# Recurrence mixer of a fused two-model block: gates and q/k square sums as rounded one-pass products, three convolution taps moved into the softmax

## What is computed

```python
h = _rmsnorm(x, norm_mix[l])
xr, gr, q, k, v, ga, gb = jnp.split(h @ w_in[l], splits, axis=-1)
xc = _centred_dwconv(xr, conv_w[l], conv_b[l])          # 4 taps along the sequence
h_fwd = _rglru_scan(xc, gates 0); h_bwd = flip(_rglru_scan(flip(xc), gates 1))
# in _rglru_scan: two block-diagonal products of xc (64x64 blocks) are the gates r and i,
#   a = exp(c*r*log_sigmoid), h[t] = a*h[t-1] + sqrt(1-a*a)*(i*xc)
y_lru = (h_fwd + h_bwd) * gelu(gr)
q = _rmsnorm(q per head) * q_norm * HEAD_DIM ** -0.5; k = _rmsnorm(k per head) * k_norm
y_att = _neighbourhood_attention(q, k, v, rel_pos_bias)  # softmax over 8 rows x 16 columns
y = sigmoid(ga) * y_lru + sigmoid(gb) * y_att
x = x + y @ w_out
```

## Time and profile before

| what | value |
|---|---|
| median of 3 runs | 2387.43 us (2387.39 to 2388.82) |
| span of the profiled execution | 2385.7 us, its first to its last instruction |
| PE, DVE, ACT, POOL busy | 99%, 54%, 42%, 7% of the span |
| one body of the loop | 51.2 us (the square sums of body 2 start at 511.07, of body 3 at 562.29) |

### The profile page before, as it was taken

How to read it: one execution, slowest core, us unless ns; L and a number is a source line. 1 busy time by engine, 2 the same in 40 slices (tenths; PEclk the granted TensorE clock), 3 DMA queues, 4 the chain that set the end, 5 groups by cost and what they waited for, 6 DMA issues and landing times.

```text
span 2385.7 us, 31197 instructions
## 1 busy us (share of the span) xinstructions
PE 2359.3 (99%) x11062; PEld 1904.2 (80%) x11062; DVE 1296.1 (54%) x1838; ACT 996.1 (42%) x1481; POOL 155.6 (7%) x137
## 2 busy tenths in 40 slices
PE   9999999999999999999999999999999999999998
PEld 8888887777777788888877778888877768888887
DVE  5444346566666734443364575555248996655424
ACT  4222224766666632232243444333234455433322
POOL 0000002434433000000000000000000000000000
PEclk9999999999999999999999999999999999999999
DMA  4333322223232232232232223333213222323321
GB/s 167 96 96 94 121 93 89 81 84 101 74 100 76 81 97 97 97 116 97 68 100 88 89 71 97 97 96 121 95 40 102 77 71 71 97 91 102 111 97 48
DMA packets 62185, 219.94 MB, mean 92 GB/s; under 512 B 7664, under 2 KB 12272, under 8 KB 62112
## 3 DMA queue, kind: packets, MB, share of 16 engines
q1 hardware_dynamic: 60944, 216.86, 28.1%
q10 hardware_dynamic: 1168, 2.12, 0.3%
HBM read 216.83 MB, written 2.12 MB: 92 GB/s over the span
## 4 chain that ended last, share of the span: by engine, by line
PE 84%; DVE 7%; ACT 5%; issue 3%; DMA 0%; ACTq 0%; DVEq 0%; SPq 0%
PE bank L1948 26%; PE bank L1950 26%; PE bank L1949 26%; DVE wL L1941 1%; ACT m_prob L242 1%; PE bank L598 1%; ACT wH L1936 1%; DVE m_prob L369 1%; PE bank L641 1%; PE bank L1042 0%; PE bank L1070 0%; PE bank L2344 0%; PE bank L2343 0%; PE bank L2342 0%; PE bank L1052 0%
## 5 line engine op out<-in xcount | busy, mean ns | idle before, releaser
L1948 PE MATMUL bank<-H,wH 128*128 128x512 f32 x2996 | 1183.4, 395 | 8.2 <-DVE L L2040 3.6
L1950 PE MATMUL bank<-H,wL 128*128 128x512 f32 x2996 | 1166.8, 389 | 0.0
L1949 PE MATMUL bank<-L,wH 128*128 128x512 f32 x2996 | 1166.5, 389 | 0.0
L1941 DVE TENSOR_TENSOR wL<-raw,wH 128x1024 fp32r<-128x1024 f32 (+1 forms) x359 | 468.5, 1312 | 610.6 <-ACT wH L1936 610.4
L1948 PEld LDWEIGHTS bank<-H,wH 128*128 128x128 f32 x2996 | 562.8, 188 | 137.5 <-issue 13.3
L1950 PEld LDWEIGHTS bank<-H,wL 128*128 128x128 f32 x2996 | 562.5, 188 | 118.7
L1949 PEld LDWEIGHTS bank<-L,wH 128*128 128x128 f32 x2996 | 562.8, 188 | 117.5 <-issue 4.1
L1936 ACT ACTIVATE wH<-raw 128x1024 fp32r<-128x1024 f32 (+1 forms) x359 | 394.9, 1108 | 215.2 <-PE bank L1950 206.0
L2158 ACT ACTIVATE H<-prod 128x512 f32 (+1 forms) x88 | 55.8, 634 | 243.8 <-DVE prod L2223 243.8
L2203 DVE TENSOR_TENSOR gate_s<-bank,rstd 128x512 f32<-128x512 f32 x88 | 60.8, 691 | 107.1 <-PE bank L1950 106.9
L2223 DVE TENSOR_TENSOR prod<-silu_g,bank 128x512 f32<-128x512 f32 x88 | 60.3, 685 | 80.1 <-PE bank L1950 74.0
(11 more groups left out here) (279 smaller groups left out, 1726.2 us busy)
## 6 DMA issues: line engine op xcount, KB each, us to landing
raw<-in_w_ffn_gu SPq DMA_DIRECT2D x88, 512.0 KB, 3.4
raw<-in_w_in SPq DMA_DIRECT2D x56, 512.0 KB, 3.6
raw<-in_w_ffn_down SPq DMA_DIRECT2D x32, 704.0 KB, 4.2
raw<-in_w_up_2a SPq DMA_DIRECT2D x44, 512.0 KB, 3.4
raw<-in_w_up_2b SPq DMA_DIRECT2D x44, 512.0 KB, 3.4
raw<-in_w_in_even SPq DMA_DIRECT2D x24, 512.0 KB, 4.4
raw<-in_w_in_odd SPq DMA_DIRECT2D x24, 512.0 KB, 3.5
raw<-in_w_down_2a SPq DMA_DIRECT2D x16, 704.0 KB, 4.2
```

The costliest lines, as they stand in the source:

```text
L1941: dve.tensor_tensor(w_l, raw_at(st, j), w_h.bitcast(F32), ALU.subtract).then_inc(S.lo_done, 1)
L1948: pe.matmul(out, w_h, xh[:, k0 + k], start=start and k == ks[0], stop=False)
L1949: pe.matmul(out, w_h, xl[:, k0 + k], start=False, stop=False)
L1950: last = pe.matmul(out, w_l, xh[:, k0 + k], start=False, stop=stop and k == ks[-1])
```

## The change

Three things. The gate products take rounded operands: ACT rounds the convolution result to `xcH` and the gate weights to `gwH`, DVE makes the remainders `xcL` and `gwL`, and each gate product becomes three one-pass products, as in `products`. The square sums become two one-pass products: ACT writes the square twice, once in float32 and once rounded (`sqH`), DVE subtracts (`sqL`), and the head matrix, which rounds exactly, is used rounded. And of the next body's convolution taps 0 and 1 now stand between `dve_scores(p, 2)` and `dve_scale(p, 2)`, tap 2 between `dve_scores(p, 3)` and `dve_scale(p, 3)`, and only tap 3 at the body's head. The new tiles lie over old ones (`over`), so DVE waits in body 0 for the gates before it writes `thb`.

```diff
+    def act_xc_high(act, p):
+        act.wait_ge(M.conv, 4 * p + 4)
+        wait(act, M.lru, 6 * p)
+        act.activation(xcH[:], xc[:], ACT.Copy).then_inc(M.gate_hi, 1)
+    def act_gw_high(act, p):
+        act.wait_ge(M.gw_loaded, 16 * p + 16)
+        wait(act, M.gab, 2 * p)
+        act.activation(gwH[:], gate_w[:], ACT.Copy).then_inc(M.gate_hi, 1)
...
                 act.activation(sqk[:, n], qk[:, n], ACT.Square).then_inc(M.sqk, 1)
+            if not first:
+                act_xc_high(act, p)
+            for n in range(2):
+                wait(act, M.qkn, 2 * p)
+                act.activation(sqH[:, n], qk[:, n], ACT.Square).then_inc(M.sqk, 1)
             slot(1)
...
             act_probT(act, p, 0)
+            act_gw_high(act, u)
             act_probs(act, p, 2)
...
         k.split_hi(act, st, 0, 4)
+        act.activation(heads1R[:], k.heads1[:], ACT.Copy).then_inc(M.gate_hi, 1)
+        act_gw_high(act, 0)
+        act_xc_high(act, 0)
...
+    def dve_xc_low(dve, p):
+        dve.wait_ge(M.gate_hi, 2 * p + 3)
+        dve.tensor_tensor(xcL[:], xc[:], xcH[:].bitcast(F32), ALU.subtract).then_inc(M.split_lo, 1)
+    def dve_gw_low(dve, p):
+        dve.wait_ge(M.gate_hi, 2 * p + 2)
+        dve.tensor_tensor(gwL[:], gate_w[:], gwH[:].bitcast(F32), ALU.subtract).then_inc(M.split_lo, 1)
+    def dve_sq_low(dve, p):
+        for n in range(2):
+            dve.wait_ge(M.sqk, 4 * p + n + 3)
+            dve.tensor_tensor(sqL[:, n], sqk[:, n], sqH[:, n].bitcast(F32), ALU.subtract).then_inc(M.split_lo, 1)
...
             if not first:
-                dve_conv(dve, p)
+                dve_conv(dve, p, (3,))
+                dve_xc_low(dve, p)
             slot(1)
...
                 dve_tail(dve, p - 1)
+            dve_sq_low(dve, p)
             if first:
                 dve_scaled(dve, 5)
...
             slot(6)
+            dve_gw_low(dve, p + 1)
             dve_lru(dve, p, 1)
             dve_scores(dve, p, 2)
+            dve_conv(dve, p + 1, (0, 1))
             dve_scale(dve, p, 2)
             dve_scores(dve, p, 3)
+            dve_conv(dve, p + 1, (2,))
             dve_scale(dve, p, 3)
...
         k.normal_dve(dve, site, 0, 3)
+        dve_gw_low(dve, 0)
+        dve_xc_low(dve, 0)
         dve_scaled(dve, 2)
...
-            pe.matmul(bank[4 + g][:], gate_w[:, 2 * d + g], xc[:], start=True, stop=True).then_inc(M.gates, 1)
+            pe.matmul(bank[4 + g][:], gwH[:, 2 * d + g], xcH[:], start=True, stop=False)
+            pe.matmul(bank[4 + g][:], gwH[:, 2 * d + g], xcL[:], start=False, stop=False)
+            pe.matmul(bank[4 + g][:], gwL[:, 2 * d + g], xcH[:], start=False, stop=True).then_inc(M.gates, 1)
...
-                pe.matmul(bank[6 + n][:], k.heads1[:], sqk[:, n], start=True, stop=True).then_inc(M.qk_stat, 1)
+                pe.matmul(bank[6 + n][:], heads1R[:], sqH[:, n], start=True, stop=False)
+                pe.matmul(bank[6 + n][:], heads1R[:], sqL[:, n], start=False, stop=True).then_inc(M.qk_stat, 1)
```

More of the change, by code:

```diff
@@ L129, in gated_recurrence_mixer @@
 def gated_recurrence_mixer(k, st, t, site):
-    bank, S, free, scratch = k.bank, k.S, k.free, k.scratch
+    bank, S, free, scratch, over = k.bank, k.S, k.free, k.scratch, k.over
     N = st.bodies
@@ L167, in gated_recurrence_mixer @@
     den = scratch("m1", "den", [8])
-    M = k.sems("m1_", "evac gab_free zeroed sqk g2 g2p gth gelu qk_stat qk_rs qk_rr qkn conv gates gate_act t2_sqrt lru ix "
+    heads1R = scratch("m1", "heads1R", [P], F32R)
+    sqH = over("m1", "sqH", "qkr", 0, [2, SEQ], F32R)
+    sqL = over("m1", "sqL", "qkn", 0, [2, SEQ], F32R)
+    xcH = over("m1", "xcH", "ti", SEQ, [SEQ], F32R)
+    xcL = over("m1", "xcL", "la", SEQ, [SEQ], F32R)
+    gwH = over("m1", "gwH", "thb", 0, [4, P], F32R)
+    gwL = over("m1", "gwL", "gate_w", 0, [4, P], F32R)
+    M = k.sems("m1_", "evac zeroed sqk g2 g2p gth gelu qk_stat qk_rs qkn conv gates gate_act t2_sqrt lru ix "
+                      "gate_hi split_lo "
                       "v_tr v_ev scores biased negmax exps rden scaled p_tr p_ev pv bias_ready run_loaded gw_loaded "
@@ L270, in body @@
             u = p + 1
+            first = isinstance(p, int) and p == 0
             def slot(n):
@@ L446, in dve_scaled, with dve_conv @@
         dve.tensor_tensor(dst, src, by, ALU.mult).then_inc(M.evac if j < 5 else M.scaled0, 1)
[L448 to L455, removed]
+    def dve_xc_low(dve, p):
[8 more added lines that the diff above has]
+            dve.tensor_tensor(sqL[:, n], sqk[:, n], sqH[:, n].bitcast(F32), ALU.subtract).then_inc(M.split_lo, 1)
+    def dve_conv(dve, p, taps=(0, 1, 2, 3)):
+        if taps[0] == 0:
+            dve.wait_ge(M.evac, PER * p + 1)
+            dve.wait_ge(M.zeroed, 2)
+            dve.tensor_scalar(xc[:], xr[:, 0:SEQ], k.colr("conv_w", p), k.colr("conv_b", p), ALU.mult, ALU.add)\
+               .then_inc(M.conv, 1)
+        for n in taps[taps[0] == 0:]:
             dve.wait_ge(M.conv, 4 * p + n)
@@ L491, in body @@
             if first:
+                dve.wait_ge(M.gates, 4)
                 dve_scaled(dve, 6)
@@ L627, in body @@
                 pe_probT(pe, p - 1, 3)
-            pe.wait_ge(M.conv, 4 * p + 4)
-            pe.wait_ge(M.gw_loaded, 16 * p + 16)
+            pe.wait_ge(M.split_lo, 4 * p + 2)
             wait(pe, M.biased, 8 * p)
@@ L635, in body @@
             for n in range(2):
-                pe.wait_ge(M.sqk, 2 * p + (n + 1))
+                pe.wait_ge(M.split_lo, 4 * p + (n + 3))
                 if n == 0:
@@ L676, in pe @@
         dense(0, 3)
+        pe.wait_ge(M.gate_hi, 1)
         body(0, True, False)
@@ L1853, in build @@
                   for n in (26, 8, 18)}
-        regions = {}
+        regions, places = {}, {}
         def free(which, tile):
@@ L1866, in scratch, with over @@
                     r[0] += n
+                    places[which, name] = r[0] - n
                     return at(f"{which}_{name}", shape, r[0] - n, dt)
             raise AssertionError((name, regions[which]))
+        def over(which, name, other, offset, shape, dt):
+            return at(f"{which}_{name}", shape, places[which, other] + offset, dt)
         bank = [ctx.enter_context(nc.psum_tensor(f"bank{b}", [P, 512], F32)) for b in range(8)]
@@ L2538, in proj_dve @@
             c.projs += 1
-        k = Names(bank=bank, S=S, free=free, scratch=scratch, sems=sems, load_unit=load_unit, split_hi=split_hi,
+        k = Names(bank=bank, S=S, free=free, scratch=scratch, over=over, sems=sems, load_unit=load_unit, split_hi=split_hi,
                   split_lo=split_lo, split_at=split_at, unit_product=unit_product, first_products=first_products, proj_start=proj_start,
```

## The result

The changed kernel takes 2398.45 us (median of 4 runs, 2396.26 to 2399.70), the kernel before in the same session 2387.85 (4 runs): a ratio of 1.0043, 95% interval 1.0032 to 1.0055, so slower by 0.4%. The forecast was 2396, slower. The profiled execution took 2396.26 with a span of 2394.4 us; the forecast span was 2394.2.

The account below looks back on a forecast made before the run. A loop body was taken as PE-bound from seam to direction 1 gates, then bound by both PE and the ACT-DVE chain. +4.5 - 0.36, +5.6 and -1.2 gave +8.5: span 2394.2, time 2396, range 2382 to 2408.

Parts of the forecast that it names:

- PE saves 1.53 a body: PE's gate and square-sum products as one-pass products: 12.3 us saved gross, 1.53 a body.
- The seam chain, -1.27 + 0.65 + 1.92: Square sums to seam: 1.27 gained by earlier gates, 0.65 paid for `gwL`, 1.92 for taps and collisions; 1.3 later.
- The queue of collisions: At the seam, DVE's taps and scalings queue with POOL's y1 products and bias additions; `wL` ends at 549.1, against 547.82.
- The bounds of the prediction: Limits on the seam's 1.92 for taps: nothing if they fit idle times, 1.0 by today's tap cost, 2.6 if POOL always leads.
- A body, +0.94: Loop body: seam 1.3 later, seam to next square sums 0.36 shorter on PE; +0.94 us a body, +5.6 over six.
- Body 0, +4.5: Body 0: roundings, `gwL` and taps bring the first seam 4.5 later, with up to 3 us waiting before the square sums.
- the 2.3 for the roundings: Body 0: `gwL`, `xcL` and rounded squares enter stretches of DVE and ACT without a pause, 2.3 us later.
- Body 7, -1.2: Body 7 has no seam work; PE saves 0.81 + 0.36 behind its square sums, the chain as much: -1.2.
- Rival 1: At the seams, collisions cost only 1.0 each: 6.4 us less, 2389.5, no change that counts; chance 0.20.
- rival 2: At the seams, DVE's idle time hides the taps and PE's saving shows: 2382.6, taps' part below 0.1; chance 0.13.
- Rival 3: At each seam, PE's new waits drop its clock, 1.7 us each, 12 us more: 2408; chance 0.17.
- has cover enough on both sides, and gives nothing back: Body's head, where three taps were taken away: enough cover on both sides, so removing them gains nothing.

Follow-up runs that it names:

- experiment 1: Changed kernel with all four convolution taps back at the body's head, both splits kept: 2386.38 us, ratio 0.9995 to the kernel before.
- experiment 2: Kernel before with only the three taps moved, gates and square sums left float32: 2402.02 us, ratio 1.0059.
- experiment 3: Changed kernel with POOL's three y1 products on 8 columns instead of 512, leaving part of y out: 2382.68 us, ratio 0.998 to the kernel before.
- experiment 5: Changed kernel with POOL's two y1 multiplications moved behind the next body's sixth bias addition: 2385.15 us, ratio 0.9989 to the kernel before.
- experiment 6: Changed kernel with body 0's gates and square sums float32 as in the kernel before, without their roundings: 2395.16 us, ratio 1.0029 to the kernel before.
- experiment 8: Changed kernel with body 0 plain, only tap 0 and `gwL` before the first scaling, y1 late, `xcH` behind slot 1: 2377.91 us, ratio 0.9955 to the kernel before.
- experiment 4: Kernel before with only the square sums split into two one-pass products: 2382.91 us, ratio 0.9979.
- experiment 10: Kernel before with only the square sums split and POOL's second and third y1 products behind its sixth bias addition: 2380.55 us, ratio 0.997.

## Why the prediction was right

It came out right in its mechanism and in nearly all steps. That the sum, 2394.2 for a span of 2394.4, is so close is luck: errors of up to 0.9 us cancel in it. The clearest reading is on the clock of body 2, on which the changed kernel's numbers are 5.14 less than in its trace.

- *PE saves 1.53 a body*: the products stand 0.23 apart, and the gates of direction 1 come 0.85 earlier, for 0.81 forecast.
- *The seam chain, -1.27 + 0.65 + 1.92*: ACT's wait before the gates is gone; POOL's sum, which follows the recurrence, starts 27.70 behind the square sums instead of 28.21. With 0.65 for `gwL` that is a gain of 1.16, where I had 1.27. From `gwL`'s start to the next instruction's it is 0.60. The taps cost 38.10 - 36.17 = 1.93 (experiment 1); in the kernel before 2.03 (experiment 2).
- *The queue of collisions, instruction by instruction*: tap 1 ended at 542.24, forecast 542.4; the scaling at 543.94, forecast 544.1; the exponentials of step 3 started at 544.86, forecast 545.0; `wL` ended at 549.17, forecast 549.1. Experiments 3 and 5 show the cause: with y1 short the seam comes 1.87 earlier, with y1 later 1.67. By the table that holds both the collisions with the taps, some 1.4, and 0.3 or more that y1 cost without them; the taps' own 0.5 stays. The bounds of the prediction knew no such split, and gave the taps behind the exponentials of step 3 too little: from there to `wL`'s end 4.1 were forecast, and 4.31 measured. That the first scaling would be near 1.3 long was too low, it is 1.59.
- *A body, +0.94*: it was +1.09, which is 0.9 us more over six bodies. The seam came 1.35 later, for 1.3, and from there to the next square sums only 0.26 was saved, for 0.36 forecast.
- *Body 0, +4.5*: the new wait is 2.54 (up to 3 was forecast), and body 1's square sums came at 463.90 instead of 459.83, 4.07 later for a forecast of 4.14. Of its terms, the 2.3 for the roundings is 2.05 by experiment 6.
- *Body 7, -1.2*: its square sums came 10.5 later, the mixer's end 9.3: -1.2.
- The rest of the kernel took 0.6 less than before, which no step of mine has, and which makes up for the bodies' excess.

*Rival 1*, collisions that cost 1.0, and *rival 2*, hidden taps, fell with experiments 1 and 2 (1.93 and 2.03). Experiment 3 ran in 2382.68, near rival 2's 2382.6, but that doesn't bear it out: y1's own cost went with the collisions there, and by the table the taps still cost about 0.5 at the seam with y1 out of the way, where that rival needed less than 0.1.

*Rival 3*, a fall of the clock at each seam, didn't come: the waits of 1.48 and 1.05 brought none in the profiled execution, nor did those of 1.00 and 1.06 in that of experiment 2, whose four runs agree within 0.5 us. The other three executions of the changed kernel have spans of 2395.7 to 2397.9, with a mean clock of 0.997 and 0.996 instead of 0.998; by my estimate that is one or two more falls of 1.7 each, and why the median lies 2.2 above the profiled execution. Where they fell no trace shows.

*What failed* is one sentence: that the head of a body "has cover enough on both sides, and gives nothing back". I had asked only whether the head had slack before. The gate split itself puts ACT's `xcH` and DVE's `xcL` between the last tap and the gates, and with four taps in front this chain is longer than PE's unit 0. So the tap move has a benefit in this kernel, about 0.5 a body, which I gave as nothing, and the kernel with the taps put back was 3 us slower than I expected of it. In the sum it hid: the tap move took the head's wait away before it could show.

## What to carry to other kernels

A place where PE waits for 0.3 us only is no slack but a second path of the same length: take PE's work away there and add to the other engines, and the sum gets worse although the bounding engine has less to do. Before an instruction is put into an idle stretch of DVE, look at what POOL runs in that stretch, and who goes first; the three taps cost 12 us here (2398.45 against experiment 1's 2386.38), most of it in collisions, and moving POOL's two products behind six additions won 13 (experiment 5). Look also at what the moved work meets in its new place: in experiment 8 it met `xcL`, at 1.1 us a body. Splitting a product into cheaper passes pays where the remainders have cover (the squares: 5 us) and not where they stand in a chain of their own (the gates, experiment 1 against 4). Once that chain is given room the gates may pay too: experiment 8, with both splits, is 2.6 us faster than experiment 10, with the squares alone, though the two differ in a tap and in body 0 as well.

## What the runs showed of the hardware

- A DVE instruction with two tensor inputs that meets a POOL product ends 0.54 and 0.56 behind POOL's end in one seam of the changed kernel, as did the product in the earlier trace rows (0.55) and `xcL` in experiment 8 (552.14 against 551.59, 0.55). Starts 0.01 us apart were followed there by either order, and by a body of 50.5 or of 49.4. The Trainium skill ("SBUF — State Buffer", section "Who interferes with whom") calls the port pair that the two engines share an exclusive lock held for a whole instruction. The trace agrees, and experiment 3 with it: 1.54 and 1.59 became 0.75 and 0.69.
- An instruction that hardly reads anything waits for POOL too: the negated maximum, 128x2, takes 0.70 beside POOL's sum in the changed kernel and ends at 545.23, 0.03 behind it; with the sum on 8 columns it takes 0.17 (experiment 3).
- Tap 0, a tensor_scalar of 128x512, took 0.54 in the seam and 1.09 at the head beside a bias addition, in experiment 1. I had bounded it from below at 0.5 and guessed no more; what decides between the two I can't tell from these runs.
- A wait of PE of 2.03 in body 0 was followed by a fall of the clock before, but one of 2.23 in experiment 4 and one of 2.02 in experiment 8, at the same place of the program, were not (windows of experiment 4, clock 1.00):

```profile
430.50:434.00 3.50, 3.50 (x20) 2.66 (x21) 3.40 (x6) 1.86 (x3) 0.00 (x0) 1.00 0.01 2
```

At the first seam waits of 2.34 and 1.03 in the changed kernel had no fall behind them (clock 1.00 from 447 to 455), waits of 2.33 and 0.83 in experiment 6 had one of 6.8 us. The length of the wait alone doesn't decide it.
